# One-hot batches run evenly through the u pass, one per six steps, with the next tile's choice in parts between them

## The chip, the cores and the metric

The kernel runs on one core of a Trainium2 chip. The metric is the device time of one execution in microseconds (us). PE is the matrix engine, DVE the vector engine, ACT the scalar engine, POOL GpSimd and SP the queue engine; each takes its instructions strictly in order.

## The reference

The reference runs two transformer layers over 512 latent and 128 context tokens. What matters here is the last part of each layer, a mixture over 16384 one-row experts (PEER):

```
q = (x @ wq).reshape(n, 8, 2, 128)
s = einsum('nhpd,hpkd->nhpk', q, subkeys)          # 8 heads, 2 halves, 128 sub-keys
sv, si = top_k(s, 16)                              # 16 of 128, 16 times for each token
cand = sv[:, :, 0, :, None] + sv[:, :, 1, None, :]
cv, ci = top_k(cand, 16)                           # 16 pairs for each head
experts = e1 * 128 + e2;  gates = softmax(cv)
u = take(u_tab, experts);  a = gelu(einsum('cd,ckd->ck', x, u))
v = take(v_tab, experts);  out = einsum('ck,ckd->cd', gates * a, v)
```

## The kernel before, in words

For the 512 latent tokens the kernel doesn't gather: it multiplies all tokens by all 16384 rows of u (the u pass), and later all weighted activations by all rows of v (the v pass). A table of gates, zero where a token didn't choose an expert, selects between them. For the 128 context tokens it gathers: 128 picks for each token, so for pick k one indirect DMA (POOL) fetches 128 rows of u, and one DVE instruction, dot(k), multiplies them by the tokens and sums up. Four buffers hold such rows, so the gather of pick k waits until dot(k-4) is done.

The u pass has 128 chunks of 128 rows each. A chunk is 8 steps, a step three 128x512 matmuls (the product of the high parts, and two that mix high and low): 24 matmuls in all, L907. Chunk n needs the low part of its weights. ACT makes the high part (high_u(n), L1211, in program order behind gelu(n-3)), and then either POOL (L1747) or DVE (L1560) subtracts it from the raw weights: low_u(n). PE waits for it at the start of chunk n (u_low_made). Chunk n also waits for gelu(n-2).

The choice is made for five tiles of 128 tokens, the context tile first, then the latent tiles 0 to 3. choose(i) is a run of some 130 DVE instructions: top 8 of each of 16 rows of scores (L1445), their places (L1450), the next 8 (L1456, L1461), the same for the pair sums, and a decoding with three-dimensional comparisons and sums (L1614 to L1652). Its softmax needs an exp from ACT (L1240). When it is done it signals `picked`. PE then turns the choice (three transposes, L920), ACT copies it out (L1265), and 32 batches follow. In each DVE builds the one-hots of four tokens (L1676), ACT weighs them by the gates (L1234), PE multiplies them (four matmuls, the spread, L931), and ACT copies the product to the table of gates (L1284), which goes to DRAM in pieces (L1228).

In the order before, the u pass is cut in sections: 11 chunks (AHEAD) while the context tile is chosen, then four times 27 (PER_TILE): 11 chunks during which DVE chooses the tile of this section, and 16 chunks (BESIDE) with a spread in each half chunk. PE turns the choice ahead of the 11th chunk, and the first spread follows behind that chunk. During the 11 chunks POOL makes the low parts, during the 16 DVE does. Behind its 11 low parts POOL waits for `picked`, issues the load of the next tile's scores and the gathers for the next 32 picks (the first four of them when the context tile is chosen).

At the end of the u pass the last eight pieces of the table are stored at once, and the v pass begins when all gelus are done. The functions that the change touches:

Of the kernel before, what the change touches and what calls it, by code (L numbers as in the profile page):

```python
# [25 lines left out]
P = 128  # L26
# [19 lines left out]
E1 = PK  # L46


AHEAD, BESIDE = 11, 16
PER_TILE = AHEAD + BESIDE  # L50
# [74 lines left out]
AFTER = E1 - AHEAD - LTILES * PER_TILE  # L125
PIECES = 8
assert AFTER >= 2 and PICKS == LTILES * BATCHES and BATCHES == 2 * BESIDE
# [3 lines left out]
def build(nc, xT, csT, consts, trig, vecs, ada, wfm, wv, wdq, wkv, wgate, wout, wq, subk, uT, urows, vtab,  # L131
# [27 lines left out]
    with ExitStack() as ctx:  # L159
# [111 lines left out]
        CV, CI, CM, CE = p_.take(PH, TOPK), p_.take(PH, TOPK), p_.take(PH, TOPK), p_.take(PH, TOPK)  # L271
        STEP, CB, CAF, CBF = p_.take(PH, TOPK), p_.take(PH, TOPK), p_.take(PH, TOPK), p_.take(PH, TOPK)
        EW = p_.take(3, P)
        EWT = p_.take(3, P)
        CSUM, CRC = p_.take(PH), p_.take(PH)
        EWC, IDX, DOT, CW = p_.take(3, P), p_.take(PICKS), p_.take(PICKS), p_.take(PICKS)
# [21 lines left out]

        WINDOWS = [AHEAD * (t > 0) + PER_TILE * max(t - 1, 0) for t in range(TILES)]
        by_pool = [n for n0 in WINDOWS for n in range(n0 + 2, n0 + AHEAD + 2)]  # L300
        by_dve = [n for n in range(E1) if n not in by_pool]
# [201 lines left out]
        def _(pe):  # L503
# [192 lines left out]
            for l in range(DEPTH):  # L696
# [200 lines left out]
                def u_chunk(n, first=0, end=DC):  # L897

                    if first == 0:
# [5 lines left out]
                    for c in range(first, end):  # L905
                        for i, (w, h) in enumerate(((0, 0), (0, 1), (1, 0))):
                            last = pe.matmul(bank(n % 2), u_part(n, w)[:, c, :], HR[:, h, c, 0:LAT],  # L907
                                             start=c == 0 and i == 0, stop=c == DC - 1 and i == 2)
                    if end == DC:
                        last.then_inc(u_used, 1)  # L910

                for n in range(AHEAD):
                    u_chunk(n)
                for t in range(LTILES):
                    n0 = AHEAD + PER_TILE * t
                    for n in range(n0, n0 + AHEAD - 1):
                        u_chunk(n)
# [4 lines left out]
                    u_chunk(n0 + AHEAD - 1)  # L922
                    for m in range(BATCHES):
                        g = BATCHES * t + m
                        pe.wait_ge(hot_ready, l * PICKS + g + 1)
                        if g == 0:
                            pe.wait_ge(s_evac, 2 * TILES * (l + 1))
                        if g >= 2:
                            pe.wait_ge(g_evac, l * PICKS + g - 1)
                        for k in range(4):  # L930
                            last = pe.matmul(bank(2 + m % 2)[:, P * k:P * k + P], HOT[:, m % 2, 1, k, :], HOT[:, m % 2, 0, k, :],  # L931
                                             start=True, stop=True)
                        last.then_inc(gmm_done, 1)
                        u_chunk(n0 + AHEAD + m // 2, DC // 2 * (m % 2), DC // 2 * (m % 2 + 1))
                for n in range(E1 - AFTER, E1):
                    u_chunk(n)
# [28 lines left out]
        def _(act):  # L965
# [135 lines left out]
            for l in range(DEPTH):  # L1101
# [122 lines left out]
                def store_gates(t, h, j):  # L1224

                    act.wait_ge(g_evac, l * PICKS + BATCHES * t + BATCHES // 2 * (h + 1))
                    rows = slice(E1 // PIECES * j, E1 // PIECES * (j + 1))
                    act.dma_start(gates[2 * t + h, :, rows, :], GB[:, h, rows, :]).then_inc(gd_out[h], 16)  # L1228

                def weigh_one_hots(t, m):  # L1230

                    act.wait_ge(hot_made, l * PICKS + BATCHES * t + m + 1)
                    for k in range(4):
                        last = nc.scalar.activation(HOT[:, m % 2, 0, k, :], HOT[:, m % 2, 0, k, :], ACT.Identity,  # L1234
                                                    scale=EWT[:, 2, 4 * m + k:4 * m + k + 1])
                    last.then_inc(hot_ready, 1)

# [18 lines left out]
                for n in range(AHEAD):  # L1256
                    gelu(n)
                    if n == AHEAD - 3:
                        exp_of_choice(0)
                for t in range(LTILES):  # L1260
                    n0 = AHEAD + PER_TILE * t
                    for k in range(AHEAD):
                        if k == AHEAD - 1:
                            act.wait_ge(tr_ready, l * LTILES + t + 1)
                            nc.scalar.copy(EWT.rearrange("p a b -> p (a b)"), PF[:, 2048:2048 + 3 * P]).then_inc(ewt_ready, 1)  # L1265
                        gelu(n0 + k)
                        if k == AHEAD - 3:
                            exp_of_choice(t + 1)
                        if t >= 1 and k < PIECES:
                            store_gates(t - 1, 1, k)  # L1270
                    weigh_one_hots(t, 0)
                    for m in range(BATCHES):
                        h = m // (BATCHES // 2)
                        if t == 0 and m == 0:
                            for k in range(2):
                                act.wait_ge(ss_out[k], (l + 1) * (16 * tiles_of(k)))
                                settled(act)
                        if m + 1 < BATCHES:
                            weigh_one_hots(t, m + 1)
                        act.wait_ge(gmm_done, l * PICKS + BATCHES * t + m + 1)  # L1280
                        if t >= 1 and m % (BATCHES // 2) == 0:
                            act.wait_ge(gd_out[h], 16 * PIECES * (l * LTILES + t))
                        at = 4 * m % (P // 2)
                        nc.scalar.copy(GB[:, h, :, at:at + 4], bank(2 + m % 2).rearrange("p (t e) -> p e t", t=4)).then_inc(g_evac, 1)  # L1284
                        if m % 2:
                            gelu(n0 + AHEAD + m // 2)
                        elif h == 1:
                            store_gates(t, 0, (m - BATCHES // 2) // 2)
                for j in range(PIECES):
                    store_gates(LTILES - 1, 1, j)  # L1290
# [13 lines left out]
                gelu(E1 - AFTER)  # L1304
                act.wait_ge(dotted, (l + 1) * PICKS)
                nc.scalar.activation(CW, DOT, ACT.Gelu).then_inc(ctx_gelu, 1)
                for n in range(E1 - AFTER + 1, E1 - 2):
                    gelu(n)
# [20 lines left out]
        def _(dve):  # L1329
# [133 lines left out]
            for l in range(DEPTH):  # L1463
# [113 lines left out]
                def choose(i, ew):  # L1577

                    def sub_keys(b):
                        return V1[:, b, :], I1U[:, b, :], s1[:, b, :], s2[:, b, :]  # L1580

                    def pairs(h):
                        return CV[:, h, :], CIU[:, h, :], c1[:, h, :], c2[:, h, :]

                    if i == 0:
                        dve.wait_ge(ss_in, 16 * (l + 1))
                    else:
                        dve.wait_ge(ss_next, 16 * (l * LTILES + i))
                    settled(dve)
                    first8(sub_keys, range(SUB))  # L1590
                    dve.drain()
                    indices8(sub_keys, range(SUB // 2))
                    indices8(sub_keys, range(SUB // 2, SUB))
                    dve.drain()
                    next8(sub_keys, range(SUB))
                    dve.drain()
                    next_indices8(sub_keys, range(SUB))
                    dve.drain()
                    nc.vector.tensor_copy(I1F, I1U)

                    for at, (a, n, w) in zip(PAIR_AT, PAIR_ROWS):
                        nc.vector.tensor_tensor(c1[:, :, at:at + n * w].rearrange("p h (a b) -> p h a b", a=n),
                                                V4[:, :, 0, a:a + n].unsqueeze(3).broadcast_to([P, PH, n, w]),
                                                V4[:, :, 1, 0:w].unsqueeze(2).broadcast_to([P, PH, n, w]), ALU.add)
                    dve.drain()
                    first8(pairs, range(PH))
                    dve.drain()
                    indices8(pairs, range(PH))
                    dve.drain()
# [399 lines left out]
```

## Time and profile before

| | us |
|---|---|
| median of 3 runs | 5225.09 (5221.78 to 5225.33) |
| the profiled execution | 5227.46 |
| its span, first to last instruction | 5225.6 |
| PE busy | 5059.2 (97%) |
| DVE busy | 3141.1 (60%) |
| ACT busy | 2038.6 (39%) |
| POOL busy | 1314.1 (25%) |

A row of a timeline gives the start, the duration, the engine, the line and operation, the tiles written and read, and how many instructions are merged in it; in brackets how long the engine was idle before and what ended that. Times are us from the start of the span. The u pass of the first layer runs from 1095.0, that of the second from 3662.2.

### The profile page before, as it was taken

The numbers are of one execution on the slowest core, as the hardware profiler recorded it, in microseconds if no ns is written. First come the engines' busy times: TensorE is split into PE (matmuls) and PEld (weight loads), VectorE is DVE, ScalarE is ACT, GpSimd is POOL, SyncE is SP. The second block draws the span as 40 slices with busy tenths as digits, with TensorE's granted clock in tenths as the row PEclk, the third lists the DMA queues.
The fourth block names the chain that finished last, engine by engine and source line by source line (L and its number), as shares of the span: only waits on it lengthen the run. The fifth ranks groups of instructions, "written<-read, shape, count | busy, mean of one in ns | idle before, by whom it ended". The sixth has DMA issues, their size and how long they took to land.

```text
span 5225.6 us, 69408 instructions
## 1 busy us (share of the span) xinstructions
PE 5059.2 (97%) x26210; PEld 4202.6 (80%) x26210; DVE 3141.1 (60%) x5589; ACT 2038.6 (39%) x3750; POOL 1314.1 (25%) x896
## 2 busy tenths in 40 slices
PE   7999999999999999999999999999999999999999
PEld 4666899787888888888876668999788888788887
DVE  2865432057887856666658654320878887566666
ACT  3344432235456442222233443322365455322222
POOL 1300233233433311111123003322434333111111
PEclk9999999999999999999999899999999999999999
DMA  7100122556777688888820001222577777888886
GB/s 271 44 26 1 46 75 69 222 210 209 260 269 266 232 288 293 290 288 292 290 84 29 26 1 56 73 69 97 186 262 245 259 273 251 287 290 290 290 290 222
DMA packets 349896, 982.02 MB, mean 188 GB/s; under 512 B 31648, under 2 KB 101408, under 8 KB 346272
## 3 DMA queue, kind: packets, MB, share of 16 engines
q1 hardware_dynamic: 216000, 553.20, 31.3%
q0 software_dynamic: 74880, 276.86, 15.7%
q10 hardware_dynamic: 58720, 148.04, 7.4%
q8 instruction: 183, 3.00, 0.2%
q14 instruction: 113, 0.93, 0.1%
HBM read 829.44 MB, written 148.54 MB: 187 GB/s over the span
## 4 chain that ended last, share of the span: by engine, by line
PE 84%; DVE 9%; issue 2%; ACT 2%; DMA 1%; DVEq 1%; POOL 0%; ACTq 0%; POOLq 0%; SPq 0%
PE PS L949 27%; PE PS L907 23%; PE PS L520 18%; PE PS L931 4%; PE PS L663 3%; PE PS L691 3%; DVE AR L1372 2%; PE PS L675 1%; PE PS L633 1%; PE PS L509 1%; DVE AR L1393 1%; DVE SM L1411 1%; DMA WR<-in_wq 1%; DVE AR L1450 0%; DVE AR L1461 0%
## 5 line engine op out<-in xcount | busy, mean ns | idle before, releaser
L949 PE MATMUL PS<-HB,VR 128*128 128x512 f32 x6144 | 1395.7, 390 | 6.9 <-DVE HB L1704 6.9
L949 PEld LDWEIGHTS PS<-HB,VR 128*128 128x128 f32 x6144 | 1154.8, 188 | 247.8 <-issue 7.7
L907 PE MATMUL PS<-HR,UR 128*128 128x512 f32 x4128 | 1028.7, 403 | 0.0
L520 PE MATMUL PS<-HR,UR 128*128 128x320 f32 (+1 forms) x5952 | 913.2, 312 | 16.6 <-POOL UR L1747 8.5
L520 PEld LDWEIGHTS PS<-HR,UR 128*128 128x128 f32 x5952 | 883.7, 189 | 47.4 <-issue 31.6
L907 PEld LDWEIGHTS PS<-HR,UR 128*128 128x128 f32 x4128 | 771.6, 191 | 174.9 <-issue 1.0
L1747 POOL TENSOR_TENSOR UR<-WR,UR 128x1024 fp32r<-128x1024 f32 x218 | 535.1, 2455 | 785.0 <-ACT UR L1099 512.5
L1296 ACT CAST VR<-HT 128x1024 fp32r<-128x1024 f32 x256 | 268.3, 1048 | 964.5 <-PE PS L949 962.0
L1691 DVE TENSOR_TENSOR VR<-HT,VR 128x1024 fp32r<-128x1024 f32 x256 | 313.7, 1225 | 465.8 <-ACT VR L1296 465.8
L907 PE MATMUL PS<-HR 128*128 128x512 f32 x2016 | 487.4, 394 | 0.0
L1676 DVE TENSOR_TENSOR AR<-AR,CN 128x1024 f32<-128x1024 f32 x256 | 325.1, 1270 | 221.1 <-PE PS L931 198.6
L1218 ACT ACTIVATE AR<-PS 128x512 f32<-128x512 f32 x256 | 153.1, 598 | 769.5 <-PE PS L907 751.9
L907 PEld LDWEIGHTS PS<-HR 128*128 128x128 f32 x2016 | 372.7, 188 | 76.4
L1234 ACT ACTIVATE AR<-AR 128x128 f32<-128x128 f32 x1024 | 327.6, 395 | 5.4 <-DVE AR L1676 5.4
L931 PEld LDWEIGHTS PS<-AR 128*128 128x128 f32 x2048 | 268.0, 191 | 47.5 <-ACT AR L1234 25.9
L931 PE MATMUL PS<-AR 128*128 128x128 f32 x2048 | 271.4, 275 | 22.4 <-ACT AR L1234 22.4
L1816 POOL DMA_INDIRECT HX<-in_vtab,AR x128 | 120.0, 938 | 687.9 <-DVE HX L1715 575.5
L1792 POOL TENSOR_TENSOR branch_split<-WR,branch_split 128x256 fp32r<-128x256 f32 x64 | 47.2, 738 | 876.2 <-ACT UR L1149 876.2
L1816 POOL DMA_INDIRECT AR<-in_urows,AR x128 | 164.6, 1286 | 270.4 <-DVE AR L1658 265.9
L1372 DVE RECIPROCAL AR<-AR 128x640 f32<-128x640 f32 (+2 forms) x40 | 172.4, 4311 | 98.5 <-ACT AR L1037 95.8
L1560 DVE TENSOR_TENSOR UR<-WR,UR 128x1024 fp32r<-128x1024 f32 x102 | 124.4, 1221 | 164.6 <-ACT UR L1211 164.5
L1411 DVE TENSOR_REDUCE SM<-PS 128x1 f32<-128x640 f32 (+3 forms) x200 | 136.7, 684 | 132.4 <-PE PS L663 129.5
(220 smaller groups left out, 6230.1 us busy)
## 6 DMA issues: line engine op xcount, KB each, us to landing
WR<-in_uT SPq DMA_DIRECT2D x256, 512.0 KB, 3.6
HT<-in_vtab SPq DMA_DIRECT2D x256, 512.0 KB, 7.2
activations<-AR ACTq DMA_DIRECT2D x256, 256.0 KB, 2.9
gates_by_expert<-AR ACTq DMA_DIRECT2D x128, 512.0 KB, 5.6
HW<-activations SPq DMA_DIRECT2D x256, 256.0 KB, 3.8
WR<-gates_by_expert SPq DMA_DIRECT2D x64, 1024.0 KB, 8.2
AR<-in_ada SPq DMA_DIRECT2D x40, 1024.0 KB, 7.6
WR<-in_wgate SPq DMA_DIRECT2D x64, 640.0 KB, 3.9
```

What stands on the lines that cost most here:

```text
L520: last = pe.matmul(out(lo, hi), part(w, c), whole(h, c, lo, hi), start=start and i == 0, stop=stop and i == 2)
L907: last = pe.matmul(bank(n % 2), u_part(n, w)[:, c, :], HR[:, h, c, 0:LAT], start=c == 0 and i == 0, stop=c == DC - 1 and i == 2)
L931: last = pe.matmul(bank(2 + m % 2)[:, P * k:P * k + P], HOT[:, m % 2, 1, k, :], HOT[:, m % 2, 0, k, :], start=True, stop=True)
L949: last = pe.matmul(bank(d), VR[:, m % 4, w, P * d:P * d + P], HB[:, (m + 1) % 3, h, :], start=m == 0 and i == 0, stop=m == E1 - 1 and i == 2)
L1234: last = nc.scalar.activation(HOT[:, m % 2, 0, k, :], HOT[:, m % 2, 0, k, :], ACT.Identity, scale=EWT[:, 2, 4 * m + k:4 * m + k + 1])
L1296: nc.scalar.copy(VR[:, m % 4, 0, :], VRAW[:, m % 4, :]).then_inc(vh_ready, 1)
L1372: nc.vector.reciprocal(RST[0:parts, 0:w], STD[0:parts, n % 2, 0:w])
L1411: nc.vector.reduce_max(MX[:, s], PF[:, at:at + n], AX.X)
L1676: nc.vector.tensor_tensor(HOT[:, m % 2], EWT[:, 0:2, 4 * m:4 * m + 4].unsqueeze(3).broadcast_to([P, 2, 4, P]), iota.unsqueeze(1).unsqueeze ...
L1691: nc.vector.tensor_tensor(VR[:, m % 4, 1, :], VRAW[:, m % 4, :], VR[:, m % 4, 0, :].bitcast(F32), ALU.subtract).then_inc(v_split, 1)
L1747: nc.gpsimd.tensor_tensor(dst, src, high.bitcast(F32), ALU.subtract).then_inc(sem_, 1)
L1816: pool.indirect_dma_start(dst, None, table, bass.IndirectOffsetOnAxis(ap=IDX.bitcast(U32)[:, k:k + 1], axis=0)).then_inc(sem_, 16)
```

## The change

Spreads are no longer bound to halves of chunks in 16 of 27 chunks. Spread g (0 to 127) stands ahead of step 200 + 6g, so from chunk 25 (LEAD) on there is one in every six steps (PACE) without a pause between tiles. The choice of a tile is cut in 28 parts, each with a drain of DVE ahead of it. The context tile and tile 0 are chosen ahead of the batches, tile t+2 during the batches of tile t, a part behind each of the batches 1 to 28. Tile t is turned 12 steps ahead of its first spread; the turned choice has two buffers. ACT copies batch g's product and then weighs batch g+1. Four dots run between the choice of the context tile and that of tile 0, four more inside the latter, the others one per batch except in six batches of each of the first three tiles, and the rest at the end. All low parts but the first two are POOL's, and POOL's gathers are placed between them by a table of when their dots are due (DOT_AT).

```diff
-AHEAD, BESIDE = 11, 16
-PER_TILE = AHEAD + BESIDE
+LEAD, PACE = 25, 6
+PARTS = 28
+TURN_AT = [(LEAD * DC if t == 0 else LEAD * DC + PACE * BATCHES * t) - 2 * PACE for t in range(LTILES)]
+WITHOUT_DOT = (21, 22, 23, 25, 26, 27)
+EARLY_DOTS = 8
+def step_of(g):
+    return LEAD * DC + PACE * g
+DOTS_OF = []
+for g in range(PICKS):
+    left = PICKS - EARLY_DOTS - sum(DOTS_OF)
+    DOTS_OF.append(0 if g < PICKS - BATCHES and g % BATCHES in WITHOUT_DOT else min(1, left))
+DOT_AT = [(10 + k // 2) * DC for k in range(EARLY_DOTS)] + [step_of(g) for g in range(PICKS) for _ in range(DOTS_OF[g])]
+DOT_AT += [step_of(PICKS - 1)] * (PICKS - len(DOT_AT))
...
-        by_pool = [n for n0 in WINDOWS for n in range(n0 + 2, n0 + AHEAD + 2)]
+        by_dve = [0, 1]
+        by_pool = [n for n in range(E1) if n not in by_dve]
...   (PE)
+                for n in range(E1):
+                    for c in range(DC):
+                        at = n * DC + c
+                        if at in TURN_AT:
+                            turn_choice(TURN_AT.index(at))
+                        g, between = divmod(at - LEAD * DC, PACE)
+                        if 0 <= g < PICKS and between == 0:
+                            spread(g)
+                        u_step(n, c)
...   (ACT, in the same order of steps)
+                                weigh_one_hots(0)
...
+                            if 0 <= g < PICKS and between == 0:
+                                copy_gates(g)
+                                if g + 1 < PICKS:
+                                    weigh_one_hots(g + 1)
+                                t, m = divmod(g, BATCHES)
+                                if t + 2 < TILES and m == 22:
+                                    exp_of_choice(t + 2)
+                                if g == PICKS - 1:
+                                    for j in range(PIECES):
+                                        store_gates(2 * LTILES - 1, j)
+                        gelu(n)
+                        if n in (7, LEAD - 5):
+                            exp_of_choice((7, LEAD - 5).index(n))
...   (DVE)
+                dots = iter(range(PICKS))
+                for _ in range(4):
+                    dot(next(dots))
+                for part in range(PARTS):
+                    choose_part(1, EW, part)
+                    if part % 6 == 5:
+                        dot(next(dots))
+                dve.nop().then_inc(picked, 1)
+                for g in range(PICKS):
+                    t, m = divmod(g, BATCHES)
+                    one_hots(g)
+                    for _ in range(DOTS_OF[g]):
+                        dot(next(dots))
+                    if t + 2 < TILES and 1 <= m <= PARTS:
+                        choose_part(t + 2, EW, m - 1)
+                        if m == PARTS:
+                            dve.nop().then_inc(picked, 1)
+                for k in dots:
+                    dot(k)
...   (POOL)
+                def dotted_rows(k):
+                    if k >= 4:
+                        pool.wait_ge(dotted, l * PICKS + k - 3)
+                    rows_of(urows, u_rows_at[k % 4], k, ur_in[k % 4])
+                def next_scores(i):
+                    pool.wait_ge(picked, l * TILES + i)
+                    pool.dma_start(S1, sub_rows[ORDER[i]]).then_inc(ss_next, 16)
+                rows = iter(range(PICKS))
+                asked = 0
+                for n in range(2, E1):
+                    low_u(n)
+                    if n == 11:
+                        next_scores(1)
+                        for _ in range(4):
+                            dotted_rows(next(rows))
+                            asked += 1
+                    while n > 11 and asked < PICKS and DOT_AT[asked - 4] // DC + 2 <= n:
+                        dotted_rows(next(rows))
+                        asked += 1
+                    for t in range(LTILES - 1):
+                        ready = LEAD if t == 0 else step_of(BATCHES * (t - 1) + PARTS) // DC + 2
+                        if n == ready:
+                            next_scores(t + 2)
```

The parts of choose_part hold the instructions of choose in their old order: 0 and 1 the first 8 of each row of scores, 2 to 7 their places, 8 and 9 the next 8, 10 to 12 their places, 13 to 18 the pairs, 19 to 26 the decoding, 27 the softmax.

## Rows read from the trace of the kernel before

**Rows 1.** The page, engines' busy time; then the waits of PE: us, times, longest.

```profile
PE 5059.2 (97%) x26210; PEld 4202.6 (80%) x26210; DVE 3141.1 (60%) x5589; ACT 2038.6 (39%) x3750; POOL 1314.1 (25%) x896
...
PE PS L931 <- ACT AR L1234: 22.4, 8, 2.8
```

**Rows 2.** Timeline of PE around the start of the batches of tile 0.

```profile
1216.32 0.91 PE L920 MATMUL PS<-CN,AR 128*128 128x128 f32 x3 [4.39 <-DVEq L1652]
1216.88 8.30 PE L907 MATMUL PS<-HR,UR 128*128 128x512 f32 x24
1227.97 1.16 PE L931 MATMUL PS<-AR 128*128 128x128 f32 x8 [2.79 <-ACT AR L1234]
1228.88 4.59 PE L907 MATMUL PS<-HR,UR 128*128 128x512 f32 x12
1233.31 1.05 PE L931 MATMUL PS<-AR 128*128 128x128 f32 x8
```

**Rows 3.** Windows: busy PE, PEld, DVE, ACT, POOL, then PE's granted clock, DMA share, GB/s.

```profile
1216.00:1220.00 4.00, 3.68 (x10) 3.02 (x11) 2.45 (x4) 0.48 (x1) 0.58 (x1) 0.50 0.67 252
```

**Rows 4.** Timeline of ACT: gelu(0), gelu(14) and gelu(15), each as its chunk ends.

```profile
1100.90 0.60 ACT L1218 ACTIVATE AR<-PS 128x512 f32<-128x512 f32 x1 [3.13 <-PE PS L907]
...
1178.64 0.60 ACT L1218 ACTIVATE AR<-PS 128x512 f32<-128x512 f32 x1 [3.94 <-PE PS L907]
...
1184.24 0.60 ACT L1218 ACTIVATE AR<-PS 128x512 f32<-128x512 f32 x1 [4.06 <-PE PS L907]
```

**Rows 5.** Timeline of POOL as the context tile's choice ends.

```profile
1152.52 2.39 POOL L1747 TENSOR_TENSOR UR<-WR,UR 128x1024 fp32r<-128x1024 f32 x1 [3.17 <-ACT UR L1211]
1154.85 0.75 POOL L1828 DMA_DIRECT2D HT<-sub_key_scores  x1
1155.90 1.01 POOL L1816 DMA_INDIRECT AR<-in_urows,AR  x1 [0.30 <-issue]
...
1159.71 0.93 POOL L1816 DMA_INDIRECT WR<-in_urows,AR  x1 [0.30 <-issue]
```

**Rows 6.** Time from issue to landing of the first gather and of the fourth.

```profile
AR<-in_urows,AR POOLq DMA_INDIRECT x1, 7.7
...
WR<-in_urows,AR POOLq DMA_INDIRECT x1, 9.2
```

**Rows 7.** Timeline of DVE: the end of the context choice, that of tile 0, a dot.

```profile
1150.02 0.29 DVE L1664 TENSOR_SCALAR AR<-AR,GN 128x128 uint32<-128x128 f32 x1
1161.27 0.29 DVE L1445 MAX8 AR<-HT 128x8 f32<-128x128 f32 x1 [10.96 <-issue]
...
1180.67 2.16 DVE L1599 CAST AR<-AR 128x256 f32<-128x256 uint32 x1
...
1191.52 2.43 DVE L1616 CAST AR<-AR 128x128 f32<-128x128 uint32 x1
...
1199.00 2.51 DVE L1625 SCALAR_TENSOR_TENSOR AR<-AR 128x128 f32<-128x128 f32 x1
...
1205.88 0.23 DVE L1635 CAST AR<-AR 128x128 f32<-128x128 uint32 x1
...
1215.95 0.29 DVE L1650 TENSOR_TENSOR AR<-AR 128x128 f32<-128x128 f32 x1
...
1218.92 1.22 DVE L1658 SCALAR_TENSOR_TENSOR AR<-AR,PS 128x1024 f32<-128x1024 f32 x1
```

**Rows 8.** The end of the u pass: ACT's last stores of gates, PE's last chunks.

```profile
1898.08 9.22 ACTq L1228 DMA_DIRECT2D gates_by_expert<-AR  x8
...
1935.94 11.36 PE L907 MATMUL PS<-HR,UR 128*128 128x512 f32 x48
1950.76 11.40 PE L949 MATMUL PS<-HB,VR 128*128 128x512 f32 x38 [3.47 <-DVE HB L1704]
```

**Rows 9.** Timeline of POOL and DVE where a one-hot and a low part meet.

```profile
1404.58 2.43 POOL L1747 TENSOR_TENSOR HR<-WR,HR 128x1024 fp32r<-128x1024 f32 x1 [3.08 <-ACT HR L1211]
...
1404.92 3.17 DVE L1676 TENSOR_TENSOR AR<-AR,CN 128x1024 f32<-128x1024 f32 x1 [3.27 <-issue]
```

More of the change, by code:

```diff
@@ L895, in _, with u_step @@
                         last.then_inc(sc_ready, 1)
-                def u_chunk(n, first=0, end=DC):
-                    if first == 0:
+                def u_step(n, c):
+                    if c == 0:
                         u_low_made(pe, l, n)
@@ L904, in u_chunk, with turn_choice @@
                             pe.wait_ge(ge_done, l * E1 + n - 1)
[L905 to L909, printed above, removed]
-                        last.then_inc(u_used, 1)
[L912 to L917, printed above, removed]
+                    for i, (w, h) in enumerate(((0, 0), (0, 1), (1, 0))):
+                        last = pe.matmul(bank(n % 2), u_part(n, w)[:, c, :], HR[:, h, c, 0:LAT],
+                                         start=c == 0 and i == 0, stop=c == DC - 1 and i == 2)
+                    if c == DC - 1:
+                        last.then_inc(u_used, 1)
+                def turn_choice(t):
                     pe.wait_ge(picked, l * TILES + t + 2)
@@ L921, in _, with spread @@
                     last.then_inc(tr_ready, 1)
[L922 to L936, printed above, removed]
+                def spread(g):
+                    pe.wait_ge(hot_ready, l * PICKS + g + 1)
+                    if g == 0:
+                        pe.wait_ge(s_evac, 2 * TILES * (l + 1))
+                    if g >= 2:
+                        pe.wait_ge(g_evac, l * PICKS + g - 1)
+                    for k in range(4):
+                        last = pe.matmul(bank(2 + g % 2)[:, P * k:P * k + P], HOT[:, g % 2, 1, k, :], HOT[:, g % 2, 0, k, :],
+                                         start=True, stop=True)
+                    last.then_inc(gmm_done, 1)
+                for n in range(E1):
[7 more added lines that the diff above has]
+                        u_step(n, c)
                 for m in range(E1):
@@ L1222, in gelu, with store_gates, weigh_one_hots, copy_turned @@
                     act.dma_start(act_rows[n], AS[:, n % 2, :]).then_inc(a_out[n % 2], 16)
-                def store_gates(t, h, j):
-                    act.wait_ge(g_evac, l * PICKS + BATCHES * t + BATCHES // 2 * (h + 1))
+                def store_gates(q, j):
+                    act.wait_ge(g_evac, l * PICKS + BATCHES // 2 * (q + 1))
                     rows = slice(E1 // PIECES * j, E1 // PIECES * (j + 1))
-                    act.dma_start(gates[2 * t + h, :, rows, :], GB[:, h, rows, :]).then_inc(gd_out[h], 16)
-                def weigh_one_hots(t, m):
-                    act.wait_ge(hot_made, l * PICKS + BATCHES * t + m + 1)
+                    act.dma_start(gates[q, :, rows, :], GB[:, q % 2, rows, :]).then_inc(gd_out[q % 2], 16)
+                def weigh_one_hots(g):
+                    t, m = divmod(g, BATCHES)
+                    act.wait_ge(hot_made, l * PICKS + g + 1)
                     for k in range(4):
-                        last = nc.scalar.activation(HOT[:, m % 2, 0, k, :], HOT[:, m % 2, 0, k, :], ACT.Identity,
-                                                    scale=EWT[:, 2, 4 * m + k:4 * m + k + 1])
+                        last = nc.scalar.activation(HOT[:, g % 2, 0, k, :], HOT[:, g % 2, 0, k, :], ACT.Identity,
+                                                    scale=EWT[:, t % 2, 2, 4 * m + k:4 * m + k + 1])
                     last.then_inc(hot_ready, 1)
+                def copy_turned(t):
+                    act.wait_ge(tr_ready, l * LTILES + t + 1)
+                    nc.scalar.copy(EWT[:, t % 2].rearrange("p a b -> p (a b)"), PF[:, 2048:2048 + 3 * P]).then_inc(ewt_ready, 1)
+                def copy_gates(g):
+                    q, m = divmod(g, BATCHES // 2)
+                    act.wait_ge(gmm_done, l * PICKS + g + 1)
+                    if m == 0 and q >= 2:
+                        act.wait_ge(gd_out[q % 2], 16 * PIECES * (l * LTILES + q // 2))
+                    nc.scalar.copy(GB[:, q % 2, :, 4 * m:4 * m + 4], bank(2 + g % 2).rearrange("p (t e) -> p e t", t=4)).then_inc(g_evac, 1)
+                    if q >= 1 and m % 2 == 0:
+                        store_gates(q - 1, m // 2)
                 def exp_of_choice(i):
@@ L1254, in _ @@
                         act.dma_start(S1, sub_rows[ORDER[0]]).then_inc(ss_in, 16)
[L1256 to L1288, printed above, removed]
@@ L1289, in _, with gelus @@
-                for j in range(PIECES):
-                    store_gates(LTILES - 1, 1, j)
+                def gelus(first, end):
+                    for n in range(first, end):
+                        for c in range(DC):
+                            at = n * DC + c
+                            if at in TURN_AT:
+                                copy_turned(TURN_AT.index(at))
+                            if at == (LEAD - 1) * DC:
+                                for k in range(2):
+                                    act.wait_ge(ss_out[k], (l + 1) * (16 * tiles_of(k)))
+                                    settled(act)
+                                weigh_one_hots(0)
+                            g, between = divmod(at - LEAD * DC, PACE)
+                            if 0 <= g < PICKS and between == 0:
[11 more added lines that the diff above has]
+                            exp_of_choice((7, LEAD - 5).index(n))
@@ L1292, in high_v @@
+                gelus(0, E1 - 3)
                 def high_v(m):
```

205 lines of the change are left out of this document (96 added, 109 removed).

## The prediction

> **What bounds the kernel now.** I read the page's busy times first, then the waits of PE, then timelines of PE, ACT, POOL and DVE in the first u pass. PE is busy for 5059.2 us of the span of 5225.6, so a change of the order is worth only what PE idles, or loses to a low clock, in the two u passes [rows 1]. From gelu(0) at 1100.90 to gelu(15) at 1184.24 a chunk takes 5.556 us (83.34 / 15), while nothing is spread [rows 4]. A spread costs PE 0.91 us (1227.97 to 1228.88), a turn some 0.25 [rows 2]. Chunks 1 to 127, 128 spreads and 4 turns would take 705.6 + 116.5 + 1.0 = 823.1 us. The pass ends at 1947.3 [rows 8], 846.4 us after gelu(0). So 23.3 us of each u pass are lost, and 46.6 of both is the most that an even order could win.
>
> Where they are lost: PE waits 4.39 us for the choice of tile 0, and the chunk behind takes 8.30 us in place of 5.6 [rows 2]; the granted clock there is 0.50, the 1.2 GHz level, after the pause [rows 3]. Then PE waits 2.79 us for the first weighed one-hots; such waits come to 22.4 us in eight [rows 1], one for each of four tiles in two layers. Behind the first of them two spreads are 5.34 us apart (1227.97 to 1233.31), although a spread and half a chunk take 0.91 + 2.78 = 3.69 [rows 2]: 1.65 lost. The rest of the 23.3 is of this kind at later tiles.
>
> **What the change takes away.** The turn stands 12 steps (12 x 0.6945 = 8.3 us) ahead of the first spread of its tile, and ACT, DVE and ACT have this time for the copy, the one-hots and the weighing, which were 2.79 us late with one chunk (at that clock 8.30, else 5.6) to hide in. With an undisturbed 8.3 us all four waits go. The wait for the choice of tile 0 goes if that choice is done by chunk 23.5. I count the whole 23.3 us per layer as won, zero to 23.3 being the bounds.
>
> **What it adds: POOL waits for dots, with low parts queued behind it.** This is the step that decides. All low parts are POOL's now, in one queue with the gathers, and gather k waits until dot(k-4) is done. By the table of due times dots 0 to 7 count as due in chunks 10 to 13, so gathers 8 and 9 stand behind low_u(14) and wait for dots 4 and 5; gathers 10 and 11 stand behind low_u(15) and wait for dots 6 and 7. But DVE runs dots 4, 5, 6 and 7 behind parts 5, 11, 17 and 23 of the choice of tile 0. So low_u(15) waits for part 11 of that choice and low_u(16) for part 23, most of its length. When is that?
>
> The context choice ended at 1150.3 [rows 7]; ten more drains at some 0.15 us (an estimate from gaps of about 0.1 between drained DVE instructions and overlaps of as much without a drain) make it 1152. POOL then issues the scores' load (0.75) and the four gathers, 1.27 apart [rows 5]: gather 0 at 1153.2, gather 3 at 1157.0. They land 7.7 and 9.2 us after issue [rows 6]: 1160.9 and 1166.2. DVE runs dots 0 to 3 ahead of the choice; dot 3 (1.22 [rows 7]) can't end before 1167.4. So the choice of tile 0 begins at about 1167.5, not 1161.27. Meanwhile low_u(12) is behind the gathers (to 1160.4), and low_u(13) behind gathers 4 and 5, which wait for dots 0 and 1 (to 1167.7, due 1167.5); both just in time.
>
> In the trace the choice took from 1161.27 to 1206.1 up to the end of what is now part 23 (the cast of L1635): 44.8 us, of which about 6.3 are three instructions that took 2.16, 2.43 and 2.51 in place of 0.2 to 0.3 beside POOL's low parts [rows 7]. Without these 38.5; with ten drains (1.5), dots 4 to 7 (4.9) and one such collision (1.9) it is 46.8. POOL mostly stands still now, so even that one may not happen (44.9), and I take the middle, 45.5 to 46. From 1167.5 that makes dot 7 end at 1213.2. Gather 11 is issued (1.3 with the signal), and low_u(16) takes 2.4 [rows 5]: chunk 16 can start at 1216.9 (all these sums are good to 2 us). It started at 1184.2, when chunk 15 ended [rows 4]. PE is 32.7 us later, in two pauses: ahead of chunk 15 (1178.6 to about 1192; part 11 and dot 5 end at 1188.7) and ahead of chunk 16. Nothing covers this: the raw weights and high parts of only three chunks can be ahead of PE, and PE has no other work. A second clock loss follows; the chunk behind the 4.39 us pause lost 2.7 [rows 2, 3], and I take this once, the one behind the first pause falling into the second.
>
> Later nothing of this kind comes: from batch 0 on, a gather stands two chunk numbers behind its dot, which POOL reaches as that dot's own chunk begins, and DVE may run two batches (10.2 us) ahead of PE. The turn of tile 0 is not late either: from 1216.9 PE needs 7.5 chunks to it, 41.7 us, and DVE only four parts and an exp.
>
> **DVE and ACT in the even part.** A batch comes every 18 matmuls and a spread: 4.17 + 0.91 = 5.08 us. DVE needs 1.22 for the one-hots, 1.22 for a dot and a 28th of a choice. The choice of tile 0 took 55.0 us (1161.27 to 1216.2 [rows 7]), a part 1.96, 4.4 in sum, under 5.08. Its heaviest parts, 20 to 26 (up to 2.6 us), mostly have no dot. DVE can fall 7 us behind before PE notices (10.2 less one-hots 1.2 and weighing 1.3, with signals). ACT has 0.6 for the copy, 1.3 for the weighing and 2 us per chunk for gelu and high part, 3.8 of 5.08. I count nothing here.
>
> But here a row speaks against the change. In the order before, one-hots seldom met a low part of POOL: these were made in the 11 chunks without batches. Where they met, at 1404.92, the one-hots took 3.17 us and not 1.22, from 0.3 us after POOL's start until 1.1 us after its end at 1407.0 [rows 9]. Now each of POOL's 24 low parts per tile may meet one. The Trainium skill, in "SBUF — State Buffer", section "Who interferes with whom", says that a DVE instruction with two SBUF inputs is fully blocked by a GpSimd instruction that reads SBUF, and the other way round; the row agrees. The Trainium skill says there too that one with at most one SBUF input outside the two-port modes isn't touched, which would spare the dots (they read PSUM).
>
> From rows: if each low part (one in 6.77 us, so 0.75 per batch) blocks DVE for 1.95 us, a batch costs DVE 4.4 + 1.46 = 5.9, which is 0.8 over the pace. In the 84 batches that have parts that is 67 us, less the 7 of slack per tile: some 46 us per layer. The 1.96 already holds the choice's own collisions, and most parts are eight-value searches that read one row; I expect half a meeting per low part, 4.4 + 0.4 to 0.7, at the pace or just below it. Zero is my value.
>
> **The end of the pass.** The last spread moves from chunk 118.5 to 120.25. ACT then issues eight stores at once, which took 9.22 us [rows 8], now ahead of gelu(120), which chunk 122 awaits 9.7 us behind the spread: late by 1 to 2 us. POOL's gathers 121 to 127 stand ahead of low_u(123) and wait for dots up to 123; with landings of 6 to 9 us the last is issued 14 to 18 us behind the spread, and chunk 123 is due at 16. I take 3 us in all, bounds 0 and 10. The gates' table has 30 us left to land. The pause of 3.47 us ahead of the v pass stays [rows 8].
>
> **Sum per layer:** +32.7 +2.7 +3 -23.3 = +15.1. Two layers: +30.2. On the profiled execution's own 5227.5 this gives 5257.7; the median of the runs was 2.4 below that execution, so 5255.
>
> **Rivals.**
> A, faster or the same: the low parts don't hang on dots 4 to 7. It decides by one number, the end of dot 7: with 23.3 won and 5.7 lost elsewhere, the change pays only if dot 7 ends before 1198, 15 us earlier than worked out. For it: only my reading of the choice's length; all of it would need the choice to begin at 1152. If the wait didn't bind at all, the time is 5225 - 46.6 + 6 = 5184. The order of the queues speaks against it. Chance 0.07, of which 0.04 faster.
> B, DVE becomes the bound through collisions with POOL: up to 46 us more per layer, half of it likelier, 5275 to 5345. For it the row of 3.17, against it the searches. 0.11.
> C, the tail: landings under the burst of stores take 10 us and more, POOL is held longer, 10 us per layer more than counted, 5270 to 5280. 0.08.
> The forecast's own case, 5238 to 5272: 0.74.
>
> **Range and chances.** 5236 to 5290 holds the forecast's case, C, and the lower part of B. Within 0.2% (10 us, about what a measurement here tells from no change) is 0.04: faster 0.04, slower 0.92.
>
> **What would show it.** Right: two pauses of PE at L907 ahead of chunks 15 and 16, about 13 and 17 us (1178 to 1192, 1200 to 1217), released by POOL's L1747 line; POOL idle before gathers 8 to 11, released by dots; no pause at the turns or the first spreads; matmuls of L907 at 231.5 ns else. Wrong: PE going through chunk 16 before 1195, waits for weighed one-hots spread over the pass (rival B), or a u pass of under 852 us.

## The result and the profile after

The changed kernel takes 5272.64 us (median of 4 runs, 5267.8 to 5278.38), the kernel before 5225.21. The ratio is 1.0091 (95% interval 1.0074 to 1.0109): slower by 0.9%, 47 us. The forecast was 5255, with a range to 5290.

The profiled execution took 5267.8 us with a span of 5266.0, so 40.4 more than before. The u pass, from the start of gelu(0) to that of gelu(127), took 846.4 and 846.3 us in the two layers before. It now takes 868.9 (1097.94 to 1966.88) and 866.3: 22.5 and 20.0 us more. The rest is -2.1 us: 3.0 less ahead of the first u pass, and 0.8 more between the two. The first stretch varies by itself: gelu(0) came between 1097.9 and 1112.4 in kernels that don't differ there.

First the page's busy times and the waits of PE in the changed kernel (us in total, times, longest), which answer to [rows 1]. PE no longer waits for weighed one-hots (22.4 us [rows 1]), nor for the choice at a turn (4.39 us in the first layer [rows 2]).

```profile
PE 5050.4 (96%) x26210; PEld 4196.1 (80%) x26210; DVE 3076.1 (58%) x5447; ACT 2038.0 (39%) x3750; POOL 1726.1 (33%) x1038
...
PE PS L923 <- POOL UR L1788: 74.1, 6, 20.1
...
PE PS L923 <- ACT AR L1237: 2.4, 2, 1.3
```

The 74.1 us are waits for low parts, which the kernel before didn't have in its u passes. The timeline of PE in the first u pass shows where they are, and answers to [rows 2]:

```profile
1170.01 5.63 PE L923 MATMUL PS<-HR 128*128 128x512 f32 x24
1188.64 8.40 PE L923 MATMUL PS<-HR,UR 128*128 128x512 f32 x24 [13.00 <-POOL UR L1788]
1215.96 8.40 PE L923 MATMUL PS<-HR,UR 128*128 128x512 f32 x24 [18.92 <-POOL UR L1788]
1224.20 5.61 PE L923 MATMUL PS<-HR 128*128 128x512 f32 x24
...
1260.26 0.49 PE L932 MATMUL PS<-CN,AR 128*128 128x128 f32 x3
...
1268.94 1.05 PE L943 MATMUL PS<-AR 128*128 128x128 f32 x8
...
1274.04 1.05 PE L943 MATMUL PS<-AR 128*128 128x128 f32 x8
...
1925.39 5.73 PE L923 MATMUL PS<-HR 128*128 128x512 f32 x24 [1.09 <-ACT AR L1237]
1936.19 14.00 PE L923 MATMUL PS<-HR,UR 128*128 128x512 f32 x48 [5.08 <-POOL UR L1788]
...
1970.31 19.92 PE L968 MATMUL PS<-HB,VR 128*128 128x512 f32 x75 [3.47 <-DVE HB L1745]
```

Chunks 15 and 16 start behind pauses of 13.0 and 18.9 us and take 8.40 in place of 5.6; the turn and the first spread come without a pause, and spreads follow each other 5.1 us apart. A window behind the second pause gives the granted clock (the columns are those of [rows 3]):

```profile
1216.00:1220.00 4.00, 4.00 (x10) 3.13 (x11) 0.06 (x1) 0.00 (x0) 4.00 (x2) 0.50 0.54 169
```

POOL in the same stretch: in brackets stands what it waited for, each time a dot (L1686), with the next low part (L1788) behind it.

```profile
1165.19 2.42 POOL L1788 TENSOR_TENSOR HR<-WR,HR 128x1024 fp32r<-128x1024 f32 x1
1174.27 0.94 POOL L1857 DMA_INDIRECT AR<-in_urows,AR  x1 [6.66 <-DVE AR L1686]
1185.27 0.94 POOL L1857 DMA_INDIRECT AR<-in_urows,AR  x1 [10.06 <-DVE AR L1686]
1186.24 2.35 POOL L1788 TENSOR_TENSOR UR<-WR,UR 128x1024 fp32r<-128x1024 f32 x1
1196.77 0.94 POOL L1857 DMA_INDIRECT HT<-in_urows,AR  x1 [8.18 <-DVE HT L1686]
1209.51 2.64 POOL L1857 DMA_INDIRECT WR<-in_urows,AR  x1 [11.80 <-DVE WR L1686]
1212.17 3.73 POOL L1788 TENSOR_TENSOR UR<-WR,UR 128x1024 fp32r<-128x1024 f32 x1
```

And DVE: dot 3, the start of the choice of tile 0, dot 7 and the two comparisons of the choice behind it.

```profile
1162.14 1.22 DVE L1686 SCALAR_TENSOR_TENSOR WR<-WR,PS 128x1024 f32<-128x1024 f32 x1 [1.26 <-DMA WR<-in_urows,AR]
...
1163.50 3.37 DVE L1471 MAX8 AR<-HT 128x8 f32<-128x128 f32 x16
...
1207.73 1.22 DVE L1686 SCALAR_TENSOR_TENSOR WR<-WR,PS 128x1024 f32<-128x1024 f32 x1
...
1209.04 2.29 DVE L1667 TENSOR_TENSOR HT<-AR,CN 128x2048 f32<-128x2048 f32 x1
1211.41 2.29 DVE L1670 TENSOR_TENSOR HT<-HT,AR 128x2048 f32<-128x2048 f32 x1
```

At the end of the pass ACT issues the eight stores, and gelu(120) stands behind them. Gather 121 is issued at 1916.41 and its dot starts at 1926.34, 9.9 us later. Low parts 123 and 124 (the pair below) wait behind gathers 125 to 127, which wait for dots. One fence for each engine, ACT, DVE, POOL:

```profile
1915.14 9.41 ACTq L1247 DMA_DIRECT2D gates_by_expert<-AR  x8
1924.65 0.60 ACT L1237 ACTIVATE AR<-PS 128x512 f32<-128x512 f32 x1 [9.54 <-PE PS L923]
```

```profile
1926.34 1.22 DVE L1686 SCALAR_TENSOR_TENSOR AR<-AR,PS 128x1024 f32<-128x1024 f32 x1 [8.34 <-DMA AR<-in_urows,AR]
```

```profile
1928.12 0.94 POOL L1857 DMA_INDIRECT AR<-in_urows,AR  x1 [7.04 <-DVE AR L1686]
...
1933.79 4.68 POOL L1788 TENSOR_TENSOR UR<-WR,UR 128x1024 fp32r<-128x1024 f32 x2
```

### The profile page after: what moved, and what is told of

Same layout as the page of the kernel before. It is cut to its first block, busy times and chain, and to the rows that moved or that the text cites. A ratio compares the mean times of both kernels' runs of the same rounds, so it can differ in the third digit from the quotient of the medians.

```text
span 5266.0 us, 69516 instructions
## 1 busy us (share of the span) xinstructions
PE 5050.4 (96%) x26210; PEld 4196.1 (80%) x26210; DVE 3076.1 (58%) x5447; ACT 2038.0 (39%) x3750; POOL 1726.1 (33%) x1038
## 4 chain that ended last, share of the span: by engine, by line
PE 82%; DVE 9%; DMA 3%; ACT 2%; issue 2%; POOL 1%; DVEq 1%; ACTq 0%; POOLq 0%; SPq 0%
PE PS L968 27%; PE PS L923 23%; PE PS L537 18%; PE PS L943 4%; PE PS L680 3%; PE PS L708 2%; DVE AR L1398 2%; PE PS L692 1%; PE PS L650 1%; PE PS L526 1%; DMA WR<-in_urows,AR 1%; POOL UR L1788 1%; DMA WR<-in_wq 1%; DVE AR L1419 1%; DVE SM L1437 1%
## 5 line engine op out<-in xcount | busy, mean ns | idle before, releaser
L923 PE MATMUL PS<-HR,UR 128*128 128x512 f32 x4128 | 1038.7, 403 | 74.1 <-POOL UR L1788 74.1
L1788 POOL TENSOR_TENSOR UR<-WR,UR 128x1024 fp32r<-128x1024 f32 x316 | 803.2, 2542 | 904.1 <-ACT UR L1118 511.8
L1697 DVE TENSOR_TENSOR AR<-AR,CN 128x1024 f32<-128x1024 f32 x256 | 426.6, 1666 | 284.3 <-PE PS L943 261.9
L1833 POOL TENSOR_TENSOR branch_split<-WR,branch_split 128x256 fp32r<-128x256 f32 x64 | 47.4, 740 | 873.9 <-ACT UR L1168 873.9
L1788 POOL TENSOR_TENSOR HR<-WR,HR 128x1024 fp32r<-128x1024 f32 x84 | 204.8, 2438 | 229.8 <-ACT HR L1230 229.8
L1269 ACT COPY AR<-PS 128x512 f32<-128x512 f32 x256 | 150.3, 587 | 331.3 <-PE PS L943 331.3
L1857 POOL DMA_INDIRECT AR<-in_urows,AR x128 | 195.5, 1528 | 73.6 <-DVE AR L1686 51.9
```

Source lines behind the costliest of these rows:

```text
L1697: nc.vector.tensor_tensor(HOT[:, g % 2], EWT[:, t % 2, 0:2, 4 * m:4 * m + 4].unsqueeze(3).broadcast_to([P, 2, 4, P]), iota.unsqueeze(1).un ...
L1788: nc.gpsimd.tensor_tensor(dst, src, high.bitcast(F32), ALU.subtract).then_inc(sem_, 1)
L1857: pool.indirect_dma_start(dst, None, table, bass.IndirectOffsetOnAxis(ap=IDX.bitcast(U32)[:, k:k + 1], axis=0)).then_inc(sem_, 16)
```

## The experiments

The table has the median and range of each kernel's runs, the ratio to the kernel before with its 95% interval, and the two u passes of the profiled execution. The kernel before was run again beside each group of experiments, and the ratios are to those runs; its medians lie between 5225.2 and 5229.9. So a difference between medians of two groups is good to about 5 us, and the u passes are the finer measure.

| kernel | us | ratio | u passes |
|---|---|---|---|
| before | 5225.21 | | 846.4, 846.3 |
| changed | 5272.64 (5267.8 to 5278.4) | 1.0091 (1.0074 to 1.0109) | 868.9, 866.3 |
| early rows moved | 5201.45 (5199.0 to 5211.1) | 0.9953 (0.9936 to 0.9969) | 831.2, 833.9 |
| only rows 10, 11 moved | 5229.15 (5226.9 to 5233.4) | 1.0005 (0.9995 to 1.0014) | 849.5, 845.9 |
| last stores apart | 5259.28 (5256.2 to 5265.0) | 1.0064 (1.0047 to 1.008) | 864.2, 864.1 |
| last gathers later | 5264.47 (5257.8 to 5267.4) | 1.0066 (1.0049 to 1.0082) | 861.2, 859.5 |
| all three | 5188.74 (5182.8 to 5200.1) | 0.9921 (0.9905 to 0.9938) | 822.2, 827.4 |
| early rows, last gathers | 5188.29 (5186.4 to 5190.4) | 0.992 (0.9903 to 0.9936) | 823.4, 827.7 |
| early rows, last gathers, first batch in chunk 24 | 5193.55 (5185.3 to 5195.8) | 0.9932 (0.9916 to 0.9949) | 826.8, 825.6 |
| early rows, last gathers, a batch per five steps | 5188.6 (5179.4 to 5192.0) | 0.992 (0.9904 to 0.9937) | 824.8, 829.6 |
| old order, turn earlier | 5270.49 (5264.7 to 5273.7) | 1.0074 (1.0057 to 1.0091) | 862.9, 862.6 |
| old order, weighing earlier | 5197.25 (5193.3 to 5200.6) | 0.994 (0.9923 to 0.9957) | 831.6, 831.0 |
| old order, that and scores earlier | 5187.96 (5182.7 to 5192.0) | 0.9921 (0.9905 to 0.9938) | 825.7, 825.8 |

**The early gathers.** Gathers 8 to 11 stand behind low parts 16, 18, 20 and 23.

```diff
-DOT_AT = [(10 + k // 2) * DC for k in range(EARLY_DOTS)] + ...
+DOT_AT = [n * DC for n in (10, 10, 11, 11, 14, 16, 18, 21)] + ...
```

> The changed kernel with one edit: POOL's gathers 8, 9, 10 and 11 stand behind low parts 16, 18, 20 and 23 and no longer behind 14, 14, 15 and 15, so that their dots (4 to 7) are done when POOL comes to them. Theory (the low parts hang on these dots): the pauses of 13.0 and 18.9 us ahead of chunks 15 and 16 and the 2.8 us of low clock behind each go, 37.5 us per layer, 75 in all: about 5197 us, no pause at the turns, the tail as it was. Rival (the choice of tile 0 is the true limit, and PE then waits for it at the turn in chunk 23): the choice ends at some 1216 and the turn comes at 1228, so this would show only if the choice is over 12 us longer beside running low parts; then 5210 or more with a wait at the turn's line. Rival (collisions of POOL's low parts with one-hots hold DVE back once PE runs without pauses): waits for weighed one-hots, and 5225 or more.

5201.45, 71 us less. The two pauses and their low clock are gone (37.7 and 32.5 us less in the u passes), and PE's waits for low parts fall from 74.1 us to this:

```profile
PE PS L923 <- POOL UR L1788: 11.3, 3, 4.4
```

Two of the three are the 4.4 us at the end of each pass. The third is new, and small: 2.4 us ahead of chunk 12 in the second layer, with a low clock behind it.

```profile
3718.37 12.88 PE L923 MATMUL PS<-HR,UR 128*128 128x512 f32 x48 [2.43 <-POOL UR L1788]
```

It is the same order once more: low_u(12) stands in POOL's queue behind the first four gathers, and these behind the end of the context tile's choice. POOL got past that wait 49.8 us behind gelu(0) in both layers of the changed kernel, and 55.4 behind it here, where five instructions of the choice took some 1.5 to 2.2 us longer beside low parts, and not two. The prediction called low_u(12) "just in time", with some 1.5 us to spare. The same wait (2.4 to 2.6 us) stands in one layer of four more of the kernels below, and explains why the second u pass of three of them takes 4 to 5 us more than the first.

So the early gathers alone turn a faster kernel into a slower one.

**Half of it**: the table reads (10, 10, 11, 11, 12, 12, 18, 21).

> The changed kernel with gathers 10 and 11 moved behind low parts 20 and 23, gathers 8 and 9 left behind low_u(14). Theory: the second pause (18.9 us) and its 2.8 us of low clock go, the first (13.0 + 2.8) stays: 5272 - 43 = 5229. Rival (the two pauses are one wait, and the first grows when the second goes): nearer 5270.

5229.15, as the theory said: 43 less. The second pause is gone and the first stands (12.2 and 12.7 us in the two layers), so the two add up. In the first layer the 2.6 us ahead of chunk 12 stand beside it.

**The last stores apart**, two behind each of gelus 120 to 123.

```diff
-                                if g == PICKS - 1:
-                                    for j in range(PIECES):
-                                        store_gates(2 * LTILES - 1, j)
                         gelu(n)
+                        if n >= E1 - 8 and n < E1 - 4:
+                            for j in range(2):
+                                store_gates(2 * LTILES - 1, 2 * (n - (E1 - 8)) + j)
```

> The changed kernel with one edit: the last eight stores of the gates' table are issued two behind each of gelus 120 to 123, not all eight ahead of gelu(120). Theory 1 (the burst both holds up gelu(120) and lengthens the landings of the last gathers, on which low_u(123) waits): the waits of 1.1 and 5.1 us and most of the 2.7 us of low clock go, 12 to 18 us in two layers: 5255 to 5260. Theory 2 (only the order of POOL's queue counts): only the 1.1 us goes, 5270.

5259.28, 13 less. In the first u pass the wait for gelu(120) is gone and that for low_u(123) falls from 5.1 to 2.4 us; gather 121 is now issued 6.0 us ahead of its dot, not 9.9. So the burst had part in both. But the u passes fell by only 4.7 and 2.2; 9.1 us less stand between the two passes of the profiled execution, and no wait of PE there explains them (the one ahead of the v pass is 3.8 us in place of 3.5).

**The last gathers later.**

```diff
-DOT_AT += [step_of(PICKS - 1)] * (PICKS - len(DOT_AT))
+DOT_AT += [(E1 - 7 + i // 2) * DC for i in range(PICKS - len(DOT_AT))]
```

> The changed kernel with one edit: gathers 122 to 127 stand two each behind low parts 123, 124 and 125, not all behind low_u(122). Both theories: low_u(123) no longer waits for dots, so the 5.1 us and the low clock behind it go, 15 us in two layers: 5257. If ACT's wait for the last dot comes too late instead, a wait of PE for gelu at chunk 127 takes their place and the gain is below 8. The 1.1 us for gelu(120) stays.

5264.47, 8 less by the medians, 7.7 and 6.8 us in the u passes, so 14.5: of the waits at the end none is left in the first layer. In the profiled run gelu(0) came 14 us later, a thing that the edit doesn't touch, and this run is the longest of the four (5267.35); whether that is why the medians show less is not shown. Against the kernel before of its own group it is 13 less (34.6 more in place of 47.4).

**All three**, and **the first and third together**.

> The changed kernel with the three edits together: gathers 8 to 11 later, the last stores apart, gathers 122 to 127 later. Theory: the terms are independent, 75 + 17.6 us less than the changed kernel, about 5180, which is what the kernel before would take without the 46.6 us that its u passes lose (5179). Rival (a hidden limit of DVE or POOL, by collisions on 24 low parts per tile): PE waits for weighed one-hots or low parts in the even part, 5195 or more.

> The changed kernel with gathers 8 to 11 behind low parts 16, 18, 20, 23 and gathers 122 to 127 two each behind low parts 123 to 125; the eight last stores stay in one burst. The kernel with all three edits had u passes of 822 and 827 us (823.1 are the bare matmuls) but waits of 11.5 and 7.2 us ahead of the v pass in place of 3.5, where DVE waited 11.7 us for the gates' table. Theory 1 (with the stores drawn out, the table's loads start among the last activations and the v pass's prefetches, and land late): the burst back, u passes of 823 to 826 and the wait 3.5 to 5, so 5178 to 5184. Theory 2 (a pass that ends earlier has to wait for the table's stores or loads however they are issued): the wait stays 7 or more, 5188.

5188.74 and 5188.29. The u passes of 822.2 and 823.4 us in the first layer are the 823.1 of matmuls alone; those of the second (827.4 and 827.7) hold the wait ahead of chunk 12. No waits for weighed one-hots appear. With the stores apart, though, PE waits ahead of the v pass for 11.5 us in the first layer and 7.2 in the second, since DVE waits for the gates' table:

```profile
PE PS L968 <- DVE HB L1745: 11.5, 1, 11.5
```

```profile
1930.51 0.69 DVE L1741 TENSOR_TENSOR HW<-HW,WR 128x512 f32<-128x512 f32 x1 [11.71 <-DMA WR<-gates_by_expert]
```

With the burst back this wait is 4.4 and 4.0, as theory 1 had it. The time is not: it is the same within the scatter, 5188 as theory 2 had it and not 5178 to 5184.

**The batches one chunk earlier** (LEAD 24, and the last gathers two per chunk behind the last spread).

> As the kernel with later gathers 8 to 11, and the whole row of batches one chunk earlier (first spread in chunk 24), with the last gathers two per chunk behind the last spread. The choice of tile 0 ended at about 1216, and the turn now comes at chunk 22.5, at about 1223: no wait if the choice is not over 7 us longer beside running low parts. Theory: the tail has 5.6 us more, the burst of stores no longer meets the last chunks: 5175 to 5182. Rival: a wait of some us at the turn with low clock behind it, 5185 or more.

5193.55: the rival. The turn waits 2.8 us for the choice in each layer, and what the tail gives is lost there. The four runs (5185.3 to 5195.8) overlap those of the kernel without this edit, so it isn't shown to be slower.

**A batch per five steps** (PACE 5, the last gathers two per chunk behind the last spread).

> As the kernel with both moves of gathers, but a spread every five steps, 15 matmuls, 4.38 us apart. DVE needs 4.4 us for one-hots, dot and a part, and 0.4 more, as one-hots took 1.67 us on average in place of 1.27 beside POOL's low parts. Theory (the port's collisions are real but DVE has slack at pace 6): at pace 5 DVE falls 0.4 us per batch behind in the 84 batches with parts, so PE waits for weighed one-hots in each of the first three tiles, some 5 to 25 us per layer, which pays for part of the tail: 5195 to 5235. Rival (DVE has much more slack than reckoned): no such waits, 5185.

5188.6: the rival. DVE still waits for PE's spreads (104.2 us in all, 262.0 at pace 6), and PE waits 0.4 us per layer for weighed one-hots. DVE had more slack than I had reckoned.

**The old order with an earlier turn.** AHEAD 12 in place of 11, and the turn two chunks ahead of the first spread.

> The kernel before, none of the change, with two small edits: sections of 28 chunks in place of 27 (12 ahead of the batches), and the turn of the choice two chunks ahead of the first spread and not one. If the 23.3 us that each u pass loses are what the rows say, the four waits of 2.79 us for the first one-hots and the low clock behind three of them go (16.1 us per layer), while the wait of 4.4 us at the first turn and its 2.7 us of low clock stay: 5225 - 32 = 5193. Rival (the losses sit in the burst of the batches itself, with a spread in each half chunk): no gain, 5225.

5270.49, which neither theory had. Every turn now waits for its choice (17.1 us in the first layer, four times up to 4.4), where only the first did, and the wait ahead of the v pass grows from 3.5 to 8.5 us; why the later choices come late in this order I did not follow up. And the wait of 2.79 us at the first spreads stays to the hundredth although the first one-hots were made by 1228.9, 14 us ahead. Timelines of ACT and of PE tell why:

```profile
1240.25 0.60 ACT L1219 ACTIVATE AR<-PS 128x512 f32<-128x512 f32 x1 [3.93 <-PE PS L907]
1240.74 1.04 ACT L1212 CAST HR<-WR 128x1024 fp32r<-128x1024 f32 x1
...
1241.68 1.27 ACT L1235 ACTIVATE AR<-AR 128x128 f32<-128x128 f32 x4
```

```profile
1234.58 5.63 PE L907 MATMUL PS<-HR 128*128 128x512 f32 x24
1243.01 1.16 PE L932 MATMUL PS<-AR 128*128 128x128 f32 x8 [2.79 <-ACT AR L1235]
```

The weighing stands in ACT's program behind the gelu of the very chunk behind which PE wants it. So PE waits each time for gelu, high part and weighing: from 1240.21, where the chunk ends, to 1243.0.

**The old order with this weighing ahead of that gelu.**

```diff
+                        if k == AHEAD - 1:
+                            weigh_one_hots(t, 0)
                         gelu(n0 + k)
...
-                    weigh_one_hots(t, 0)
                     for m in range(BATCHES):
```

> The kernel before with one edit on ACT: the first weighing of one-hots of each tile stands ahead of the gelu of the last chunk before the batches, not behind it. Theory, formed on the last run (the wait of 2.79 us at each first spread is ACT's order: the weighing stood behind a gelu, which waits for the end of the very chunk behind which PE wants the one-hots): the four waits and the low clock behind three of them go, 16 us per layer: 5228 - 32 = 5196. Rival, the prediction's own reason (the time from the turn to the first spread is too short for copy, one-hots and weighing): no gain, as this edit gives no more time.

5197.25, 29 less than the kernel before beside it (5226.64), with one instruction group moved. The four waits of 2.79 us in the first layer shrink to none at tile 0 and 0.6 at the others:

```profile
PE PS L931 <- ACT AR L1234: 1.8, 3, 0.6
```

At tile 0 the weighing (ACT) now ends before the chunk does, and the spread (PE) follows without a pause:

```profile
1219.84 1.28 ACT L1234 ACTIVATE AR<-AR 128x128 f32<-128x128 f32 x4 [1.29 <-DVE AR L1677]
```

```profile
1225.58 1.05 PE L931 MATMUL PS<-AR 128*128 128x128 f32 x8
```

**And the scores of tile 0 earlier.** POOL loads them, and issues the first four gathers, ahead of low_u(12).

> The kernel before with that edit and one on POOL: the load of tile 0's scores and the first four gathers stand ahead of low_u(12), not behind it, so the choice of tile 0 starts 4.3 us earlier. Theory: the first turn's wait of 4.4 us and the 2.7 us of low clock behind it go as well; with this all 23.3 us per layer are won back in the old order: 5228 - 46.6 = 5182. Rival (the first turn's wait depends on something else than the start of the choice, such as ACT's exp): 5196 as without this edit.

5187.96. The wait at the first turn is gone, and the u passes (825.7, 825.8) are within 3 us of the matmuls alone. Its time is that of the best version of the even order (5188.3), within the scatter.

## Why the prediction was right, and where it was off

**What bounds the kernel, and what can be won (23.3 us per layer): right.** Kernels of both orders come to it: the best of each take 822 to 826 us in the first layer and 826 to 830 in the second, where the prediction put 823.1.

**The wait of POOL for dots (+32.7 us): right in place, cause and size.** Measured by PE's start of chunk 16 against gelu(0) it is 118.0 less 83.3, so 34.7, and 34.2 in the second layer. Dot 7 ended 111.0 us behind gelu(0), and 112.3 was predicted. From there to chunk 16 it took 7.0 us, not 3.7: gather and low part took 2.64 and 3.73 beside DVE's comparisons at 1209.04 and 1211.41, where those ahead of them took some 0.95 and 2.4. Moving the gathers shows the cause.

**The low clock (+2.7): right.** 8.40 less 5.60 is 2.8 at chunk 16. The granted clock was 0.50, the 1.2 GHz level, from 1216 to 1220, behind a pause of 18.9 us; it had been so behind one of 4.4 [rows 3]. In the second layer the chunk took 7.20, so the loss was 1.6, behind a pause of 20.1 us: a longer pause didn't cost more.

**The end of the pass (+3, bounds 0 and 10): mis-sized.** The pauses were 1.1 and 5.1 us and the low clock took 2.6, in sum 8.8 in the first layer; in the second 1.3, 4.4 and 2.2, so 7.9. The working had landings of 6 to 9 us for the gathers that meet the stores; the one that decided took 9.9. With the stores apart it was 6.0. The working also left out the low clock behind the pause. This was the mechanism of rival C at half its price: 5 to 6 us per layer more than counted, where C had 10. The total of 5272.64 lies in the range given to C (5270 to 5280), and 0.6 outside the forecast's own case, because the first term and the scatter added the rest.

**The gain (-23.3): the size right, one reason wrong.** The prediction said that the one-hots were late because there was too little time from the turn, and that 8.3 us would suffice. The two experiments in the old order show that more time alone doesn't help. The wait comes from ACT's order: with more time and the old place of the weighing it stayed at 2.79, with the new place and no more time it fell to 0.6 or nothing. The change removes it by weighing batch 0 ahead of gelu(24). So that the whole gain came is partly luck: the order was right for another reason than the one given.

**DVE and ACT in the even part (0): right.** One-hots took 1.67 us on average in place of 1.27, 0.40 per batch, as [rows 9] had warned; the prediction had reckoned 0.4 to 0.7 for the whole batch. PE waited for none of them. The Trainium skill ("SBUF — State Buffer", "Who interferes with whom") says that a DVE instruction with two SBUF inputs and a GpSimd instruction that reads SBUF contend for ports that one of them holds alone. The trace agrees, and in both directions. In the first layer 57 of the 128 one-hots began well inside a low part, and each of them ended 1.07 to 1.09 us behind the end of that low part; the others took 1.2. Another 31 low parts began while a one-hot ran, took 2.8 us or more, and ended 2.25 to 2.28 us behind that one-hot's end. So the later of the two did nearly all of its work behind the earlier one. One meeting of each kind, POOL's rows first:

```profile
1284.52 2.41 POOL L1788 TENSOR_TENSOR HR<-WR,HR 128x1024 fp32r<-128x1024 f32 x1 [1.85 <-ACT HR L1230]
...
1291.02 3.29 POOL L1788 TENSOR_TENSOR UR<-WR,UR 128x1024 fp32r<-128x1024 f32 x1 [2.18 <-ACT UR L1230]
```

```profile
1285.20 2.82 DVE L1697 TENSOR_TENSOR AR<-AR,CN 128x1024 f32<-128x1024 f32 x1 [0.45 <-PE PS L943]
...
1290.82 1.22 DVE L1697 TENSOR_TENSOR AR<-AR,CN 128x1024 f32<-128x1024 f32 x1
```

The dots, which read PSUM, stayed at 1.21. So the expected half a meeting per low part came true (57 in some 100). Rival B had the mechanism and the wrong consequence.

The sum per layer was +15.1, and 22.5 and 20.0 came. Of the difference of 6.2 on average, 5 to 6 are the tail and 1.5 to 2 the first term; the low clock of the second layer took 1.1 less than counted. Rival A is refuted: 5184 is near what the kernel takes once both waits are moved away (5188), not what it takes as it stands. The 47 us by medians are 5 more than the u passes hold, and 7 more than the two profiled executions differ by; the runs of the two kernels lie 6.5 and 10.6 us apart, and I leave this open.

## What to carry to other kernels

When instructions of two kinds share an in-order queue, write beside each wait which instruction stands behind it and when that one is due: here a table of due times had four dots in chunks 12 and 13, where 14, 16, 18 and 21 fit, and PE stood still for 32 us per layer. When a wait is the same to the hundredth each time it occurs, look for a fixed order of instructions between the two engines before giving it more time. And price a rebuild against the one-line repairs of each wait that it is to remove: two moves in the old order gave what the rebuilt one gives at its best.

## What was not expected of the hardware

Under eight stores of 512 KB issued at once, the store queue of ACT was busy for 9.4 us and an indirect gather of 128 rows landed after 9.9 us, where the medians over the kernel before were 5.7 and 6.5 and the same gather took 6.0 with the stores apart. A one-hot instruction took 0.4 us more on average once all low parts ran on POOL. A low part on POOL took 2.52 us on average in place of 2.47, and 3.73 at worst in the stretch shown.
